# A hybrid encoder trunk on one core: RG-LRU gates without reciprocals and in another order, and another signal for a stage's last weight slot

## The reference, cut to what matters

```
xc = causal_dwconv(xb, conv_w) + conv_b
r, i = sigmoid(xc @ gate_w[0] + gate_b[0]), sigmoid(xc @ gate_w[1] + gate_b[1])   # 8 blocks of 64
log_a = -8 * r * softplus(-lam)
a = exp(log_a)
u = xc * i * sqrt(-expm1(2 * log_a))          # sqrt(1 - a*a)
h[t] = a[t] * h[t-1] + u[t]
y = h * gelu(gate_in)
```

## Time and profile before

| | us |
|---|---|
| median of 3 runs | 3311.98 (3310.5 to 3312.21) |
| the profiled execution | 3308.34 |
| its span | 3306.6 |
| TensorE busy | 3144.0 (95%) |
| GpSimd busy | 1760.3 (53%) |
| VectorE busy | 1568.8 (47%) |
| ScalarE busy | 722.4 (22%) |
| mean granted TensorE clock | 0.974 |

### The profile page before, as it was taken

The page is one execution under the profiler, slowest core; times in us unless marked ns, Lnnn a source line. Parts: engine busy times, 40 slices in busy tenths (PEclk is TensorE's granted clock), DMA queues, the critical chain, the costliest instruction groups (busy, mean ns, idle before and its releaser), DMA issues.

```text
span 3306.6 us, 42241 instructions
## 1 busy us (share of the span) xinstructions
PE 3144.0 (95%) x14648; PEld 2546.1 (77%) x14648; DVE 1568.8 (47%) x1950; ACT 722.4 (22%) x1293; POOL 1760.3 (53%) x1003
## 2 busy tenths in 40 slices
PE   8999999899999899999999999998999998999997
PEld 7888765678888777888788887656888887778886
DVE  3332455855537435333343324558555474453323
ACT  2110213322221222110021102143222212221101
POOL 6666452433346655666666674424333567456663
PEclk9999999999999999999999999998999999999998
DMA  4223221211122222333222332111111223223231
GB/s 155 95 95 102 86 83 39 70 45 58 52 83 94 97 78 76 96 100 99 93 90 95 98 105 93 60 50 64 51 52 52 90 89 109 71 77 99 97 102 57
DMA packets 78992, 272.63 MB, mean 82 GB/s; under 512 B 8304, under 2 KB 12688, under 8 KB 78864
## 3 DMA queue, kind: packets, MB, share of 16 engines
q1 hardware_dynamic: 73632, 264.27, 24.4%
q10 hardware_dynamic: 5088, 5.96, 0.6%
q0 software_dynamic: 144, 0.66, 0.1%
HBM read 268.73 MB, written 2.12 MB: 82 GB/s over the span
## 4 chain that ended last, share of the span: by engine, by line
PE 84%; DVE 8%; issue 5%; POOL 2%; ACT 1%; DMA 0%; DVEq 0%; POOLq 0%; SPq 0%; ACTq 0%
PE acc L551 73%; PE aux L551 10%; DVE dc L1688 1%; DVE sq_sum L1590 1%; POOL wh L534 1%; DVE dc L1686 1%; POOL wl L536 1%; PE aux L760 1%; DVE xf L1575 0%; DVE xf L1578 0%; DVE y_sum L1584 0%; ACT tmp L1188 0%; DVE lc L1749 0%; DVE li L1748 0%; DMA raw<-in_stream 0%
## 5 line engine op out<-in xcount | busy, mean ns | idle before, releaser
L534 POOL TENSOR_SCALAR wh<-raw 128x1024 fp32r<-128x1024 f32 x496 | 541.0, 1091 | 1462.8 <-PE acc L551 741.4
L536 POOL TENSOR_TENSOR wl<-raw,wh 128x1024 fp32r<-128x1024 f32 x496 | 1220.2, 2460 | 41.4
L551 PE MATMUL acc<-xh,wh 128*128 128x512 f32 x2432 | 994.8, 409 | 65.6 <-POOL wl L536 27.5
L551 PE MATMUL acc<-xh,wl 128*128 128x512 f32 x2432 | 961.6, 395 | 0.0
L551 PE MATMUL acc<-xl,wh 128*128 128x512 f32 x2432 | 929.6, 392 | 0.0
L551 PEld LDWEIGHTS acc<-xh,wh 128*128 128x128 f32 x2432 | 465.1, 191 | 197.2 <-issue 56.8
L551 PEld LDWEIGHTS acc<-xh,wl 128*128 128x128 f32 x2432 | 466.3, 192 | 91.3 <-issue 2.9
L551 PEld LDWEIGHTS acc<-xl,wh 128*128 128x128 f32 x2432 | 460.1, 189 | 99.1
L551 PE MATMUL acc<-hh,wh 128*128 128x512 f32 x704 | 273.9, 389 | 0.0
L551 PE MATMUL acc<-hh,wl 128*128 128x512 f32 x704 | 273.9, 389 | 0.0
L551 PE MATMUL acc<-hl,wh 128*128 128x512 f32 x704 | 273.9, 389 | 0.0
(11 more groups left out here) (266 smaller groups left out, 3764.4 us busy)
## 6 DMA issues: line engine op xcount, KB each, us to landing
raw<-in_stream SPq DMA_DIRECT2D x496, 512.0 KB, 3.4
xf<-in_xT SPq DMA_DIRECT2D x2, 1024.0 KB, 9.7
bias<-rel_scratch ACTq DMA_DIRECT2D x2, 1024.0 KB, 5.5
mraw<-in_memT ACTq DMA_DIRECT2D x2, 1024.0 KB, 5.5
out_xT<-xf SPq DMA_DIRECT2D x8, 256.0 KB, 2.0
gate_w<-in_gate_w ACTq DMA_DIRECT2D x2, 512.0 KB, 3.5
const<-in_const POOLq DMA_DIRECT2D x1, 640.0 KB, 7.8
sc<-in_ba_w ACTq DMA_DIRECT2D x2, 256.0 KB, 2.6
```

The costliest lines, as they stand in the source:

```text
L534: pool.tensor_scalar(wh[:, s, :], raw[:, s, :], 1.0, 0.0, ALU.mult, ALU.add).then_inc(hi_step, 1)
L536: pool.tensor_tensor(wl[:, s, :], raw[:, s, :], wh[:, s, :].bitcast(F32), ALU.subtract).then_inc(unit_split, 1)
L551: return pe.matmul(out, w, x, start=start, stop=stop, skip_group_check=True)
```

## The change

The RG-LRU: ScalarE squares a into `tmp[2 + p % 2]`, and VectorE forms q = (1 + a*a) * s in one operation, since 1 - a*a = (1 + a*a) * tanh(-log_a); the scale of the sqrt becomes 0.25. i and s stay in `aux` in place of `li` and `lr`. `gate_w` is loaded in the first normalisation of the layer, with the other loads of the mixer, into an address that `ycl` takes over later.

Order: TensorE makes the gates of p = 0 and 1 at once, without the wait for the attention's last `ycl`, then mixer tiles 0 and 1, gates 2 and 3, and then 20 parts. The number of parts ahead of each later step is as before. ScalarE evicts tiles 0 and 1 after p = 1, tiles 2 and 3 after the four sqrt, and tiles 4, 5 and 6 ahead of `y_hi0`, `y_hi1` and `y_hi3`. VectorE does head 0's `conv1` after `xi1` and `conv0` after `xi2`. The other convolutions stay.

The weight slot: where a stage ends in `norm_sums` with nothing beside, `unit_begun` is raised by the first sum product and not by the first product of the next stage.

```
+LRU_DRAIN = {0: 20, 1: 24, 3: 28}
...
-    return {1: only(n, "g_last", "decay_min", "kd_arg", "conv1"), 2: only(n, "decay", "silu1", "conv0"),
+    return {1: only(n, "g_last", "decay_min", "kd_arg") + (only(n, "conv1") if n else []),
+            2: only(n, "decay", "silu1") + (only(n, "conv0") if n else []),
...                                                                       (first_four)
-                        if k == 0 and n == 0:
+                        if k == 0 and n == 0 and norm == 2:
                             first.then_inc(unit_begun, 1)
...                                                                       (first_by_arrival)
-                        first = mm(acc[:, n, :], wh[:, n, c], xh[:, k, :], k == 0, False)
-                        if k == 0 and n == 0:
-                            first.then_inc(unit_begun, 1)
+                        mm(acc[:, n, :], wh[:, n, c], xh[:, k, :], k == 0, False)
...                                                                       (norm_sums)
-                    mm(aux[:, c, 0:1], sq_sum[:, c * P:(c + 1) * P], mean_w[:, 0:1], True, False)
+                    first = mm(aux[:, c, 0:1], sq_sum[:, c * P:(c + 1) * P], mean_w[:, 0:1], True, False)
+                    if c == 0 and beside is None:
+                        first.then_inc(unit_begun, 1)
...                                                                       (attention, rg_lru on TensorE)
-                pe.wait_ge(yc_lo.sem, yc_lo.at(l, KB))
...
+                pe.wait_ge(lru_dve.sem, lru_dve.after(l, f"conv{KB - 1}"))
+                pe.wait_ge(mix_par_loaded[0], l * 16 + 16)
                 for p in range(KB):
-                    fill(l, PARTS[0])
-                    if p == 0:
-                        pe.wait_ge(lru_dve.sem, lru_dve.after(l, f"conv{KB - 1}"))
-                        pe.wait_ge(mix_par_loaded[0], l * 16 + 16)
                     if p >= 2:
-                        pe.wait_ge(lru_act.sem, lru_act.after(l, f"i{p - 2}"))
+                        pe.wait_ge(lru_dve.sem, lru_dve.after(l, f"xi{p - 2}"))
                     for g in range(2):
                         mm(aux[:, 2 * (p % 2) + g, :], gate_w[:, g, p, :], lc[:, p, :]).then_inc(lru_gates.sem, 1)
-                fill(l, FILL_LRU)
-                pe.wait_ge(lru_act.sem, lru_act.after(l, "i3"))
+                    if p == 1:
+                        pe.wait_ge(yc_lo.sem, yc_lo.at(l, KB - 1))
+                        fill(l, PARTS[0])
+                        pe.wait_ge(yc_lo.sem, yc_lo.at(l, KB))
+                        fill(l, PARTS[0])
+                fill(l, 2 * PARTS[0] + FILL_LRU)
+                pe.wait_ge(lru_dve.sem, lru_dve.after(l, "xi3"))
...                                                                       (start of TensorE)
+            pe.sem_inc(unit_begun, 1)
...                                                                       (rg_lru on ScalarE)
                 for p in range(KB):
-                    mixer_tile(l, p)
-                    for g, dst in enumerate((lr, li)):
-                        act.wait_ge(lru_gates.sem, lru_gates.at(l, 2 * p + g + 1))
-                        done(fn(dst[:, p, :], aux[:, 2 * (p % 2) + g, :], ACT.Tanh, scale=0.5,
-                                bias=lam[:, 6 + g, p:p + 1]), f"{'ri'[g]}{p}")
+                    r_in, i_in = (aux[:, 2 * (p % 2) + g, :] for g in range(2))
+                    act.wait_ge(lru_gates.sem, lru_gates.at(l, 2 * p + 1))
+                    done(fn(lr[:, p, :], r_in, ACT.Tanh, scale=0.5, bias=lam[:, 6, p:p + 1]), f"r{p}")
+                    act.wait_ge(lru_gates.sem, lru_gates.at(l, 2 * p + 2))
+                    done(fn(i_in, i_in, ACT.Tanh, scale=0.5, bias=lam[:, 7, p:p + 1]), f"i{p}")
                     own(f"r{p}")
                     done(fn(lx[:, p, :], lr[:, p, :], ACT.Exp, ...), f"a{p}")
-                    done(fn(lr[:, p, :], lr[:, p, :], ACT.Tanh, ...), f"s{p}")
+                    done(fn(r_in, lr[:, p, :], ACT.Tanh, ...), f"s{p}")
+                    own(f"a{p}")
+                    done(fn(tmp[2 + p % 2][:, :], lx[:, p, :], ACT.Square), f"sq{p}")
+                    if p == 1:
+                        mixer_tile(l, 0)
+                        mixer_tile(l, 1)
                 for p in range(KB):
                     dve(f"q{p}")
-                    done(fn(lr[:, p, :], lr[:, p, :], ACT.Sqrt, scale=0.5, bias=eps_0[:, :]), f"q{p}")
-                drain(l, 4 * PARTS[0] + FILL_LRU)
+                    done(fn(lr[:, p, :], lr[:, p, :], ACT.Sqrt, scale=0.25, bias=eps_0[:, :]), f"q{p}")
+                mixer_tile(l, 2)
+                mixer_tile(l, 3)
                 for p in range(KB):
+                    if p in LRU_DRAIN:
+                        drain(l, LRU_DRAIN[p])
                     dve(f"y{p}")
                     done(fn(ych[:, p, :], tmp[p % 2][:, :], ACT.Copy), f"y_hi{p}")
...                                                                       (rg_lru on VectorE)
                 for p in range(KB):
-                    act_(f"s{p}")
-                    if p:
-                        own(f"q{p - 1}")
-                    link(ts_(tmp[0][:, :], lr[:, p, :], 1.0, None, ALU.add))
-                    link(dve.reciprocal(tmp[0][:, :], tmp[0][:, :]))
-                    done(tt_(lr[:, p, :], lr[:, p, :], tmp[0][:, :], ALU.mult), f"q{p}")
-                    done(stt_(li[:, p, :], li[:, p, :], 1.0, lc[:, p, :], ALU.add, ALU.mult), f"xi{p}")
+                    act_(f"sq{p}")
+                    done(stt_(lr[:, p, :], tmp[2 + p % 2][:, :], 1.0, aux[:, 2 * (p % 2), :], ALU.add, ALU.mult), f"q{p}")
+                    done(stt_(li[:, p, :], aux[:, 2 * (p % 2) + 1, :], 1.0, lc[:, p, :], ALU.add, ALU.mult), f"xi{p}")
+                    if 1 <= p <= 2:
+                        head_conv(l, 0, 2 - p)
```

More of the change, by code:

```diff
@@ L48 @@
 LRU_C = 8.0
-LAYER_LINKS = 197
+LAYER_LINKS = 189
 UNIT = 1024
@@ L299 @@
 DN_ACT = delta_steps(lambda n: only(n, "kg"), act_beside, act_core, act_tail, lambda p: [(HN, "std")] + only(p, "z_th", "y_hi"))
-DN_DVE = delta_steps(lambda n: only(n, "m", "c0", "kd"), dve_beside, dve_core, dve_tail,
+DN_DVE = only(0, "conv1", "conv0") + delta_steps(lambda n: only(n, "m", "c0", "kd"), dve_beside, dve_core, dve_tail,
                      lambda p: [(HN, "rate")] + only(p, "z_gate", "o_normed", "y", "y_lo"))
@@ L311 @@
 LRU_ACT = [(f"{x}{p}",) for p in range(KB) for x in ("g_sq", "g_th")]
-LRU_ACT += [(f"{x}{p}",) for p in range(KB) for x in ("r", "i", "a", "s")]
+LRU_ACT += [(f"{x}{p}",) for p in range(KB) for x in ("r", "i", "a", "s", "sq")]
 LRU_ACT += [(f"q{p}",) for p in range(KB)] + [(f"y_hi{p}",) for p in range(KB)]
@@ L355, in trunk @@
             ych = sb("ych", [P, 2 * KB, SEQ], F32R, mix)
+            with ExitStack() as lru_w:
+                gate_w = sb("gate_w", [P, 2, KB, P], F32, lru_w)
             ycl = sb("ycl", [P, 2 * KB, SEQ], F32R, mix)
@@ L379, in trunk @@
                 li = sb("li", [P, KB, SEQ], F32, lru)
-                gate_w = sb("gate_w", [P, 2, KB, P], F32, lru)
             with ExitStack() as dn:
@@ L1267, in attention @@
                 out_copy(KB - 1)
-                act.dma_start(gate_w[:, :, :, :], gate_w_d[l]).then_inc(mix_par_loaded[0], 16)
                 for n in range(HA * CH, LRU_BESIDE_END):
@@ L1296, in rg_lru @@
                 for p in range(KB):
[L1297 to L1301 removed]
+                    r_in, i_in = (aux[:, 2 * (p % 2) + g, :] for g in range(2))
[3 more added lines that the diff above has]
+                    done(fn(i_in, i_in, ACT.Tanh, scale=0.5, bias=lam[:, 7, p:p + 1]), f"i{p}")
                     own(f"r{p}")
                     done(fn(lx[:, p, :], lr[:, p, :], ACT.Exp, scale=lam[:, 4, p:p + 1], bias=lam[:, 4, p:p + 1]), f"a{p}")
[L1305 removed]
+                    done(fn(r_in, lr[:, p, :], ACT.Tanh, scale=lam[:, 5, p:p + 1], bias=lam[:, 5, p:p + 1]), f"s{p}")
+                    own(f"a{p}")
[3 more added lines that the diff above has]
+                        mixer_tile(l, 1)
                 for p in range(KB):
                     dve(f"q{p}")
[L1308 to L1309 removed]
+                    done(fn(lr[:, p, :], lr[:, p, :], ACT.Sqrt, scale=0.25, bias=eps_0[:, :]), f"q{p}")
+                mixer_tile(l, 2)
+                mixer_tile(l, 3)
                 for p in range(KB):
+                    if p in LRU_DRAIN:
+                        drain(l, LRU_DRAIN[p])
                     dve(f"y{p}")
@@ L1507, in mixer_loads @@
             def mixer_loads(l):
+                act.dma_start(gate_w[:, :, :, :], gate_w_d[l]).then_inc(mix_par_loaded[0], 16)
                 act.dma_start(ba_w, ba_w_d[l]).then_inc(mix_par_loaded[1], 16)
@@ L1738, in rg_lru @@
                 for p in range(KB):
-                    act_(f"s{p}")
-                    if p:
-                        own(f"q{p - 1}")
-                    link(ts_(tmp[0][:, :], lr[:, p, :], 1.0, None, ALU.add))
```

(20 more changed lines are left out.)

## The result

The changed kernel takes 3270.33 us (median of 4 runs, 3268.11 to 3272.3) against 3311.24 for the kernel before (4 runs, 3310.47 to 3312.21): ratio 0.9876, interval 0.9859 to 0.9893. The profiled execution took 3269.72 us, its span 3267.9, 38.7 less than before.

A forecast was written before the change was run, and what follows sets the result against it. TensorE's waits for VectorE's `ycl` and GpSimd's `wl`, plus half clock behind longer gaps, bound the kernel. LRU 31.6 plus slot 10.2 gave 41.8 us off 3308.34; with the difference to the median, 3271, range 3260 to 3286.

The forecast's parts named there:

- The term of the LRU: LRU stage of both layers' mixers: 15.8 us saved a layer, 31.6 in all, bounds 20 and 10 a layer.
- `y_lo3` and the first `up` tile: Layer 0's LRU end: `y_lo3` at 628.3, TensorE waits 2.5 us instead of 9.1, `up` starts 8.3 us earlier.
- `q` and `xi` at 0.69, never blocked: VectorE in the LRU: with one PSUM input these operations take 0.69 us, never 2.88 beside GpSimd.
- The rates: Head 0: TensorE's gap before the rates about 0.9 us instead of 4.57, resuming at 644.9, not 658.74.
- Clock behind the first gap: Behind the 2.5 us gap at 626: clock may fall, losing 1.6 to 3 us, part hidden; half of 2 taken.
- Clock behind the rates: Head 0, behind the 0.9 us gap: no half clock expected, granted clock 1.00, another 2.95 us saved.
- Later heads keep their order and their fills; nothing is won or lost there: Mixer heads after head 0: order and fills unchanged, so no gain or loss in time.
- The slot: Four stage starts: waits for `wl` save 9.9 us, five normalisations cost 1.7, clock adds 2: 10.2 us.
- 1: Rival, LRU tail stays late: `up` tile about 632, clock falls, second gap 3 us; saves 25 us, 3287; chance 0.17.
- 4: Rival, VectorE's LRU chain loses the port every time: `y_lo3` at 663, kernel slower, 3342; chance 0.02.
- 2: Rival, all hides in the LRU: `y_lo3` by 626, no half clock; saves 51 us, 3261; chance 0.09.
- 3: Rival, GpSimd's subtraction blocks the statistics: up to 2.2 us in five places, 11 against 9.9; 3281; chance 0.10.

The follow-up runs named there:

- lru_alone: The changed kernel without the `unit_begun` edits, so with the old weight slot signal; 3284.11 us, ratio 0.9919 to the kernel before.
- slot_alone: The kernel before with only the `unit_begun` edits, LRU untouched; 3298.56 us, ratio 0.996 to the kernel before.
- reciprocals_back: The changed kernel in its new order, with q again s / (1 + s) by add, reciprocal and product, without the square; 3284.94 us.
- drain_together: The changed kernel with ScalarE evicting tiles 4, 5 and 6 together ahead of `y_hi0`; 3276.89 us.
- gates_in_sbuf: The changed kernel with s and i written to SBUF instead of staying in PSUM, so `q` and `xi` have two SBUF inputs; 3276.39 us.
- convs_back: The changed kernel with head 0's `conv1` and `conv0` back between the decay and the norms; 3278.31 us.
- after_again: The changed kernel once more, unedited, run beside later variants; 3270.86 us, ratio 0.9877 to the kernel before.
- proj_and_conv2_late: The changed kernel with head 1's k projection ahead of the first `up` tiles, and head 0's `conv2` and `up` evictions behind the rates; 3258.17 us.

## Why the prediction was right, step by step

The time and the mechanisms were right, and the sum nearly (38.7 us of span against 41.8). The term of the LRU was too large, 15.8 a layer where 13.1 came, and what was off in it is the clock. Two pieces of luck hid this in the median; they are told under "The rest".

- **Where it would be won**: right. The waits that fell are those that the prediction placed: for `wl` 9.6 us, for `ycl` 15.1, for `rates` 9.2 to 1.2. The wait for `y_sum` grew by 1.7, as forecast. `lru_alone` and `slot_alone` add up.
- **`y_lo3` and the first `up` tile**: right. From the end of `values` to the `up` tile 48.8 us were forecast (579.75 to 628.5), 49.3 measured (577.2 to 626.51); the gap 2.5 against 3.06. Two of the last ten operations were at 2.88, as many as forecast, and a third at 1.35. The moved `conv0` met GpSimd and ended at 602.6, as forecast (605, in the forecast's time, which runs 2.5 ahead). `reciprocals_back` and `drain_together` show that both edits carry this step.
- **`q` and `xi` at 0.69, never blocked**: right, 8 of 8, each with GpSimd at work beside it; in `gates_in_sbuf` five of the eight were held up, by 0.4 to 2.2 us.
- **The rates**: right; 0.9 forecast, 0.59 measured, and `convs_back` shows that the moved convolutions bring it.
- **Clock behind the first gap: wrong in size.** The forecast took "half of 2", on the ground that part hides beneath VectorE's chain. The 6 us at 0.51 cost 2.9, and nothing hid them: VectorE, with fewer collisions than forecast, had its `up` tiles done at 640.0 and stood 5.14 idle ahead of the rates; TensorE was late. The step times of the forecast had TensorE's norm sums at full clock.
- **Clock behind the rates: wrong in size.** Forecast 1.00, measured 0.70 over 5.6 us, 1.7 lost, behind a gap of only 0.59. One gap of 1.49 with full clock behind it was too little to go by.
- **"Later heads keep their order and their fills; nothing is won or lost there"**: wrong twice, with opposite signs. Head 1's gap kept its length and lost its half clock (2.7 won), and a dip at 770 to 780 came in (1.6 lost), in both layers and in `after_again` too. Per layer: 16.8 forecast behind the rates, less 0.5 (later `up` tile), 2.9 and 1.7 (clock), plus 0.3 (shorter gap), is 12.0; plus 2.7, less 1.6 is 13.1, and 13.2 and 13.0 were measured. The term was 15.8.
- **The slot**: right by its parts. Waits 9.9 as forecast, clock 1.7 for 2, the sums 1.8 for 1.7; 9.8 in its own places against 10.2. `y_sum` went to 1.03 and TensorE's wait for it from 0.81 to 1.15, the forecast 0.35, and over the program from 6.6 to 8.3. That the lead through the five normalisations comes to -1.8 is closer than it deserves, as single places give -1.4 to +1.0. The statistics' product stayed at 0.16; the subtraction ended at 378.18, 1.35 ahead of the statistics, where 0.3 was forecast.
- **The rest**: 2.8 us of lead that no step names, 1.8 of it clock at 2110 to 2130. So the LRU's 5.4 too much was half paid elsewhere, which is luck. A second piece of luck lies between the executions: the forecast carried over that the profiled execution before was 3.6 under its median, and the one after is only 0.6 under its own. This 3.0 stands against the 3.1 that the saving fell short by, so 3270.33 against 3271 is nearer than the terms deserve.
- **Rivals**: 1 and 4 fell by the `ycl` wait of 3.06 (they need 6 and more); 2 fell by the same wait and the clock; 3's mechanism acts where the signal comes 1.9 us later, at 1.3 us a place (15.2 less 8.7, over five) and not 2.2. The Trainium skill, "SBUF — State Buffer", section "Who interferes with whom", has a VectorE instruction with two SBUF inputs wait for a GpSimd instruction that reads SBUF, and one with a single SBUF input, outside the two-port modes, not. The 1.57 against 0.16 and the 0.68 of eight `q` and `xi` agree.

What stays open: why the dip at 770 to 780 is there after and not before, and what decides whether a gap of 2.84 is followed by half or by full clock; no run here took that apart. It limits every difference of a few us above, since an edit also moves where the clock falls elsewhere.

## What to carry to other kernels

When one engine's chain holds another up at two places in a row, cover both before judging: a fill at the first place alone moved the wait to the second (3269.49), an earlier product at the second alone bought idle time (3271.86), both bought 12.7 us. Put the half clock behind a gap that remains into the step times of what follows, at its full length, unless the engine that is waited for is the later one. And a signal that starts a GpSimd split is worth placing by which VectorE operations will meet it: 1.9 us later cost 4.3 us over five places. Before a difference of a few us is put down to an edit, look where in the two traces it arises: 5 of the 13.9 us of `reciprocals_back` lie where nothing was edited.

## What the runs showed of the hardware

- Gaps of the same length and place were followed by different clocks: 2.85 us by 0.50 in the kernel before, 2.84 by 1.00 after, 2.84 by 0.50 in layer 0 of `proj_and_conv2_late` and 2.86 by 1.00 in layer 1 of the same execution; the 3.06 gap by 0.51 (again 0.53), and a 3.08 one by 0.72 in `lru_alone`; the 0.64 ahead of the rates in `proj_and_conv2_late` by 0.70 and by 1.00. What the profiled neighbourhood of one gap shows is not a rule for the next.
- The LRU's scan, with both inputs in SBUF, took 1.22 us in all eight instances of the kernel before and all eight of the one after, but no subtraction of GpSimd was running beside any of these 16, since the operations ahead of them had met it, or it had not begun. In `gates_in_sbuf` it took 3.30 us in two of layer 0's four, both begun 0.5 us behind a subtraction's start (the first at 609.87 against 609.38). So it is blocked as the others are, and the prediction's "none of 8" was not a test. VectorE's timeline there:

```profile
609.87 3.30 DVE L1761 TENSOR_TENSOR_SCAN lc<-xf,li 128x512 f32<-128x512 f32 x1
```

- A block lasts until the other's instruction ends, however short the blocked one is: a product of 128x4, begun at 379.05, took 1.57 us for 0.16 and ended with GpSimd's subtraction at 380.60.
- One SBUF input alone did not keep an operation free: the TENSOR_SCALAR of `conv0` took 2.07 us for 0.48 beside GpSimd's subtraction, while `q` and `xi`, with their other input in PSUM, stayed at 0.67 to 0.69.
